# Merge gate products in three split passes, recurrent roots in pairs, and splits moved, in a two-layer diffusion step

## The reference, cut to what is computed

```
h = rmsnorm(x) * (1 + scale1) + shift1
q, k, v, xr, gr, ga, gb = split(h @ w_in)
att = attention(q, k, v)                  # 8 heads of 128; latent: band plus context keys; a sink
xc = conv4(xr)
for d in (forward, backward):
    r = sigmoid(block_diag(xc, wa) + ba);  i = sigmoid(block_diag(xc, wx) + bx)
    log_a = -8 * r * softplus(-lambda)
    u = sqrt(1 - exp(2 * log_a)) * (i * xc)
    y_d = scan(h = exp(log_a) * h + u)
merged = sigmoid(ga) * (att @ w_attn_proj) + sigmoid(gb) * ((gelu(gr) * (y_0 + y_1)) @ w_rnn_proj)
x = x + gate1 * (merged @ w_out)
x = x + gate2 * moe(rmsnorm(x) * (1 + scale2) + shift2)      # 16 experts, top 2 in one group
```

## Time and profile before

| | us |
|---|---|
| median of 3 runs | 1554.89 (1554.48 to 1556.72) |
| the profiled execution, its own time | 1553.74 |
| its span, first to last instruction | 1551.9 |
| mean granted clock of TensorE | 0.992 of full speed |

### The profile page before, as it was taken

The page is one execution under the profiler, slowest core; times in us unless marked ns, Lnnn a source line. Parts: engine busy times, 40 slices in busy tenths (PEclk is TensorE's granted clock), DMA queues, the critical chain, the costliest instruction groups (busy, mean ns, idle before and its releaser), DMA issues.

```text
span 1551.9 us, 19505 instructions
## 1 busy us (share of the span) xinstructions
PE 1493.8 (96%) x7383; PEld 1192.0 (77%) x7383; DVE 1116.6 (72%) x1717; ACT 921.5 (59%) x1176; POOL 161.2 (10%) x218
## 2 busy tenths in 40 slices
PE   6999999999998999999999999999999899999996
PEld 4699866669875788888769988666999478888885
DVE  4447656774646999999873665677564789999986
ACT  1323569982224887778752355999321578778774
POOL 0100012200011000000240000221000201000002
PEclk9999999999999999999999999999999999999999
DMA  9455433216547999999855644112340799999983
GB/s 350 172 193 198 154 112 105 75 57 217 217 167 277 361 402 408 408 408 406 318 193 173 214 165 164 63 64 89 134 141 32 301 354 407 413 411 410 407 348 123
DMA packets 132708, 373.01 MB, mean 240 GB/s; under 512 B 9216, under 2 KB 12672, under 8 KB 132608
## 3 DMA queue, kind: packets, MB, share of 16 engines
q1 hardware_dynamic: 113728, 326.57, 55.9%
q0 software_dynamic: 10432, 25.18, 4.6%
q10 hardware_dynamic: 8448, 19.94, 3.3%
HBM read 351.71 MB, written 19.94 MB: 239 GB/s over the span
## 4 chain that ended last, share of the span: by engine, by line
PE 81%; DVE 6%; ACT 5%; DMA 4%; issue 3%; POOL 1%; SPq 0%; POOLq 0%; ACTq 0%; DVEq 0%
PE bank L551 24%; PE bank L864 21%; PE bank L870 11%; PE bank L540 10%; PE bank L561 2%; DMA ring<-in_w_ada 2%; PE bank L836 2%; PE bank L749 2%; PE bank L722 1%; PE bank L577 1%; PE bank L659 1%; PE bank L654 1%; PE bank L570 1%; PE bank L908 1%; PE bank L973 1%
## 5 line engine op out<-in xcount | busy, mean ns | idle before, releaser
L1915 DVE TENSOR_TENSOR spot_low<-spot,piece_high 128x2048 fp32r<-128x2048 f32 x192 | 433.5, 2287 | 31.5 <-ACT piece_high L1279 30.1
L1279 ACT ACTIVATE piece_high<-spot 128x2048 fp32r<-128x2048 f32 x192 | 366.6, 1917 | 42.4 <-PE bank L870 40.2
L864 PE MATMUL bank<-piece_high,ga_r 128*128 128x512 f32 x768 | 308.7, 402 | 2.9 <-ACT ga_r L1296 1.4
L864 PE MATMUL bank<-spot_low,ga_r 128*128 128x512 f32 x768 | 301.7, 393 | 0.0
L870 PE MATMUL bank<-piece_high,ga_r 128*128 128x512 f32 x768 | 210.7, 396 | 0.0
L551 PE MATMUL bank<-parts_r,ga_r 128*128 128x384 f32 x768 | 202.6, 345 | 0.0
L540 PE MATMUL bank<-hT,ring 128*128 128x384 f32 x544 | 184.9, 494 | 4.3 <-ACT ga L1221 2.3
L864 PEld LDWEIGHTS bank<-piece_high,ga_r 128*128 128x128 f32 x768 | 144.3, 188 | 37.8 <-ACT ga_r L1284 2.2
L870 PEld LDWEIGHTS bank<-piece_high,ga_r 128*128 128x128 f32 x768 | 144.3, 188 | 34.6
L864 PEld LDWEIGHTS bank<-spot_low,ga_r 128*128 128x128 f32 x768 | 144.6, 188 | 30.7
L540 PEld LDWEIGHTS bank<-hT,ring 128*128 128x128 f32 x544 | 102.1, 193 | 71.0 <-issue 3.9
(11 more groups left out here) (317 smaller groups left out, 2337.4 us busy)
## 6 DMA issues: line engine op xcount, KB each, us to landing
spot<-in_w_gate_up SPq DMA_DIRECT2D x128, 1024.0 KB, 8.0
spot<-in_w_down SPq DMA_DIRECT2D x64, 1024.0 KB, 8.0
ring<-in_w_ada SPq DMA_DIRECT2D x24, 2048.0 KB, 8.6
ring<-in_w_in SPq DMA_DIRECT2D x22, 2048.0 KB, 8.2
expert_rows<-gb ACTq DMA_DIRECT2D x28, 512.0 KB, 6.9
ring<-in_w_attn_proj SPq DMA_DIRECT2D x4, 2048.0 KB, 7.9
ring<-in_w_rnn_proj SPq DMA_DIRECT2D x4, 2048.0 KB, 12.5
ring<-in_w_out SPq DMA_DIRECT2D x4, 2048.0 KB, 7.8
```

The lines of the kernel that those rows point to most:

```text
L864: pe.matmul(out[n], high[:, 2 * q + k, :], w[:, k, n * 512:(n + 1) * 512], start=(q == 0 and k == 0 and i == 0), stop=False)
L1279: ac.activation(highs[p % HIGHS], spots[u], ACT.Copy).then_inc(S("piece_high"), 1)
L1915: ve.tensor_tensor(spots_low[u], spots[u], highs[p % HIGHS].bitcast(F32), ALU.subtract)\
```

## The change

- ga and gb join `SPLIT` between gr and ap, so all 24 products of the loop are split products. high_part and low_part are now issued in every iteration of the loop, two products ahead, the first two of ap included.
- The high parts get new homes, listed one by one in `HIGH_HOMES`: three pieces of the tile gb (G0 to G2), spare, two pieces of the tile xc (X0, X1, free once 6 and 12 scans are done), and three pieces of `parts` (A0 to A2). A high part waits for the product that last used its home.
- The root goes by 1 - a*a = (1 + a)^2 * tanh(-log_a / 2), so sqrt = (1 + a) * sqrt(tanh(.)). The square on ACT and one_minus_square on DVE go; the factor (a + 1) is applied in scan, after the root.
- The roots are taken in pairs: `lru_root(i-10)` and `lru_root(i-9)` in even iterations only.
- The scan is moved from number i-9 to number i-10 in iteration i; the last two are made in the ap stage.
- Attention's output is split into `hT_r` and `qT_r` (its own place), as is the merged output. The recurrent output is no longer split in scan but by `rnn_split` in the ap stage, into `parts_r[:, 1]` and `gr_r`.

```diff
-SPLIT = [(kind, n) for kind in ("q", "xr", "gr", "ap", "rp", "wo") for n in range(KT)]
+SPLIT = [(kind, n) for kind in ("q", "xr", "gr", "ga", "gb", "ap", "rp", "wo") for n in range(KT)]
-LATE_HIGHS = 4
+LATE = 5 * KT
+HIGH_HOMES = (["G0", "G1", "G2"] * 2 + ["G0", "G1"]
+              + ["G2", "spare", "G2", "spare", "G2", "X0", "spare", "X0"]
+              + ["X1", "spare", "X0"] + (["A0", "A1", "A2", "spare"] * KT)[:3 * KT - 3])
+SCANS_OF_HOME = {"X0": 6, "X1": 12}
+def home_user_ahead(at):
+    same = [b for b in range(EARLY, at) if HIGH_HOMES[b - EARLY] == HIGH_HOMES[at - EARLY]]
+    return same[-1] if same else None
+RNN_SPLIT_AT = {2: (0,), 3: (1, 2), 4: (3,), 5: (4, 5), 6: (6,), 7: (7,)}
...
 PE, loop
-                    if kind == "gr":
-                        split_product(l, kind, i, parts_r[:, 0], parts_r[:, 1])
-                    else:
-                        product((l, kind, i % KT), s, i % 4, h_all)
+                    split_product(l, kind, i % KT, parts_r[:, 0], parts_r[:, 1])
...
-                for name, high, low in (("ap", parts_r[:, 0], parts_r[:, 1]), ("rp", qT_r, gr_r),
-                                        ("wo", parts_r[:, 0], parts_r[:, 1])):
+                for name, high, low in (("ap", hT_r, qT_r), ("rp", parts_r[:, 1], gr_r), ("wo", hT_r, qT_r)):
...
 ACT, high_part
-                    if at >= EARLY + LATE_HIGHS:
-                        ac.wait_ge(S("gemm_done"), G_AT[(l, *SPLIT[at - LATE_HIGHS])] + 1)
-                    elif at > EARLY:
+                    if at >= EARLY and home_user_ahead(at):
+                        ac.wait_ge(S("gemm_done"), G_AT[(l, *SPLIT[home_user_ahead(at)])] + 1)
+                    elif at >= EARLY and HIGH_HOMES[at - EARLY] in SCANS_OF_HOME:
+                        ac.wait_ge(S("lru_used"), l * 16 + SCANS_OF_HOME[HIGH_HOMES[at - EARLY]])
+                    elif at >= LATE:
                         ac.wait_ge(S("gemm_done"), G_AT[(l, "gb", KT - 1)] + 1)
...
 ACT, lru_tables and lru_root
-                    link(ac.activation(a, a, ACT.Exp, bias=c_log[0], scale=c_log[0]))
-                    if m:
-                        ac.wait_ge(S("lru_square"), m)
-                    ac.activation(a2, a, ACT.Square).then_inc(S("lru_act"), 1)
+                    ac.activation(a, a, ACT.Exp, bias=c_log[0], scale=c_log[0]).then_inc(S("lru_act"), 1)
-                    ac.wait_ge(S("lru_square"), l * 16 + n + 1)
+                    ac.wait_ge(S("lru_act"), l * 16 + n + 1)
...
 ACT, loop and after it
-                    if i == 3 * KT - 1:
-                        high_part(EARLY)
-                    if i > KT:
+                    if i > KT and i % 2 == 0:
+                        lru_root(i - KT - 2)
                         lru_root(i - KT - 1)
-                    if i + AHEAD < KT:
-                        high_part(2 * KT + i + AHEAD)
+                    high_part(2 * KT + i + AHEAD)
...
-                high_part(EARLY + 1)
                 lru_tables(15)
+                high_part(LATE + AHEAD)
+                lru_root(14)
                 lru_root(15)
...
 DVE, scan
-                    link(ve.scalar_tensor_tensor(ti, ti, 1.0, xc[:, j, :], ALU.add, ALU.mult))
+                    ve.wait_ge(S("lru_act"), m + 1)
+                    ve.scalar_tensor_tensor(ti, ti, 1.0, xc[:, j, :], ALU.add, ALU.mult)
                     ve.wait_ge(S("root_ready"), m + 1)
+                    link(ve.scalar_tensor_tensor(th, a, 1.0, th, ALU.add, ALU.mult))
                     link(ve.tensor_tensor(th, th, ti, ALU.mult))
...
-                        halves(qT_r[:, j, :], gr_r[:, j, :], gr[:, j, :]).then_inc(S("rnn_ready"), 1)
...
+                def rnn_split(j):
+                    if j == 0:
+                        ve.wait_ge(S("gemm_done"), G_AT[(l, "gb", KT - 1)] + 1)
+                    halves(parts_r[:, 1, j, :], gr_r[:, j, :], gr[:, j, :]).then_inc(S("rnn_ready"), 1)
...
 DVE, loop and ap stage
-                    if i + AHEAD < KT:
-                        low_part(2 * KT + i + AHEAD)
-                    if i > KT:
-                        one_minus_square(i - KT - 1)
-                        scan(i - KT - 1)
-                low_part(EARLY)
+                    low_part(2 * KT + i + AHEAD)
+                    if i > KT + 1:
+                        scan(i - KT - 2)
                 att_split(HEADS - 1)
-                low_part(EARLY + 1)
-                one_minus_square(15)
-                scan(15)
                 for n in range(KT):
-                    low_part(EARLY + n + AHEAD)
+                    low_part(LATE + n + AHEAD)
+                    if n < 2:
+                        scan(14 + n)
+                    for j in RNN_SPLIT_AT.get(n, ()):
+                        rnn_split(j)
```

More of the change, by code:

```diff
@@ L293, in build @@
         actT = gaf[:, 2048:2560].rearrange("p (k c) -> p k c", k=4)
-        parts_r, qT_r, gr_r = sb_r("parts"), sb_r("qT"), sb_r("gr")
+        parts_r, qT_r, gr_r, hT_r = sb_r("parts"), sb_r("qT"), sb_r("gr"), sb_r("hT")
         flat_r = lambda name: sb_r(name)[:, :, :].rearrange("p k t -> p (k t)")
-        hTf, xcf, gaf_r, gbf_r, spare_r = flat_r("hT"), flat_r("xc"), flat_r("ga"), flat_r("gb"), sb_r("spare")
+        xcf, gaf_r, gbf_r, spare_r = flat_r("xc"), flat_r("ga"), flat_r("gb"), sb_r("spare")
         flat_parts_r = parts_r[:, :, :, :].rearrange("p i k t -> p (i k t)")
@@ L301, in build @@
         w_parts = [(part(gaf_r, i), part(gbf_r, i)) for i in range(PAIRS_OF_PARTS)]
-        late_high = [part(spare_r, 0)] + [part(hTf, i) for i in range(LATE_HIGHS - 1)]
+        high_home = {"spare": part(spare_r, 0)}
+        for i in range(3):
+            high_home[f"G{i}"], high_home[f"A{i}"] = part(gbf_r, i), part(flat_parts_r, i)
+        for i in range(2):
+            high_home[f"X{i}"] = part(xcf, i)
         ring_r = sb_r("ring")
@@ L383, in w_high_part @@
             at = SPLIT_AT[kind, n]
-            return w_parts[at % PAIRS_OF_PARTS][0] if at < EARLY else late_high[at % LATE_HIGHS]
+            return w_parts[at % PAIRS_OF_PARTS][0] if at < EARLY else high_home[HIGH_HOMES[at - EARLY]]
         def w_low_part(l, kind, n):
@@ L729, in _ @@
                     kind = ("gr", "ga", "gb")[i // KT]
-                    if i % 4 == 0 and kind != "gr":
-                        s = weights(l, kind + str(i % KT // 4))
                     scores(i)
-                    if kind == "gr":
-                        split_product(l, kind, i, parts_r[:, 0], parts_r[:, 1])
-                    else:
-                        product((l, kind, i % KT), s, i % 4, h_all)
+                    split_product(l, kind, i % KT, parts_r[:, 0], parts_r[:, 1])
                     if i % 4 == 0 and i <= KT:
@@ L1071, in high_part @@
                     ac.wait_ge(S(f"w_loaded{s}"), 16 * (use + 1))
[L1072 to L1074 removed]
+                    if at >= EARLY and home_user_ahead(at):
[3 more added lines that the diff above has]
+                    elif at >= LATE:
                         ac.wait_ge(S("gemm_done"), G_AT[(l, "gb", KT - 1)] + 1)
[L1076 removed]
+                    elif at >= PAIRS_OF_PARTS:
                         ac.wait_ge(S("gemm_done"), G_AT[(l, *SPLIT[at - PAIRS_OF_PARTS])] + 1)
@@ L1229, in _ @@
                 att_copy(23)
-                high_part(EARLY + 1)
                 lru_tables(15)
+                high_part(LATE + AHEAD)
+                lru_root(14)
                 lru_root(15)
-                for at in range(EARLY, len(SPLIT)):
-                    if at + AHEAD < len(SPLIT):
+                for at in range(LATE, len(SPLIT)):
+                    if LATE < at < len(SPLIT) - AHEAD:
                         high_part(at + AHEAD)
-                    if at == EARLY:
+                    if at == LATE:
                         ada_copy(l, 10)
@@ L1485, in softplus @@
                 ve.tensor_scalar(sp_(6), sp_(2), -4.0, None, ALU.mult)
-                ve.tensor_scalar(sp_(7), sp_(2), 4.0, None, ALU.mult)
+                ve.tensor_scalar(sp_(7), sp_(2), 2.0, None, ALU.mult)
                 ve.tensor_scalar(hb[:, 0, :, :], vec[:, :, 1, 0:16], 0.5, None, ALU.mult)
@@ L1638, in softmax_norm @@
                         .then_inc(S("probs_ready"), 1)
[L1640 to L1644, removed]
                 def scan(n):
@@ L1698, in att_split @@
                     if h == 0:
-                        ve.wait_ge(S("gemm_done"), G_AT[(l, "gr", KT - 1)] + 1)
-                    halves(parts_r[:, 0, h, :], parts_r[:, 1, h, :], qT[:, h, :]).then_inc(S("att_split"), 1)
+                        ve.wait_ge(S("gemm_done"), G_AT[(l, "vl", 1)] + 1)
+                    halves(hT_r[:, h, :], qT_r[:, h, :], qT[:, h, :]).then_inc(S("att_split"), 1)
+                def rnn_split(j):
+                    if j == 0:
+                        ve.wait_ge(S("gemm_done"), G_AT[(l, "gb", KT - 1)] + 1)
+                    halves(parts_r[:, 1, j, :], gr_r[:, j, :], gr[:, j, :]).then_inc(S("rnn_ready"), 1)
```

(6 more changed lines are left out.)

## The result

The changed kernel takes 1600.95 us (median of 4 runs, 1599.95 to 1603.35), the kernel before on the same chip 1555.81 (4 runs, 1554.48 to 1558.61): ratio 1.0299, 95% interval 1.0280 to 1.0317. It is slower by 45 us; 1600 was predicted. The profiled run has a span of 1599.0 us against 1551.9.

A forecast was written before the change was run, and what follows sets the result against it. PE was taken to set the pace, ACT right behind. Per layer +27 - 1.8 + 0.5 - 2.0 - 0.5 = +23, two layers +46, on 1553.7 gives 1600 us; range 1578 to 1640.

The forecast's parts named there:

- Part 3: Loop from i = 10: gate functions wait for the later scan, so ACT and DVE take turns; loss 27 us per layer.
- and behind low_part: DVE's queue in the loop: the scan runs behind the weights' remainder as well as one iteration later; no separate size.
- The covers: PE's about 7.0 us per iteration fits into 10.2, busy about 70%; ap-stage scans and splits, 29 of 34 us, are hidden.
- The recurrent output's split: Moved to ap, hidden until its last split, behind rp 0's remainder; between 1 us gain and 2 loss, gain 0.5 taken.
- The gain in i = 8 and 9: Two loop iterations with no wait for a scan yet, where the cheaper product was to gain 1.8 us per layer.
- The splits in 6 and 7: Weights of ga 0 and 1 split ahead of a softmax_max on DVE: 1.1 us, of which 0.5 was charged.
- The tail behind exps(23): From the last exps to the first ap product: 10.25 us was to become about 8.2, a gain of 2.0.
- The signs: Profile after: gate functions idle 2 us or more, exps 10.6 and 9.5 to 10 apart, about 32 fewer table loads.
- (a): Rival, loop: engines overlap after all and PE sets the pace, 1520 us; needs a round below 8.1 us; chance 0.12.
- (b): Rival, even iterations: both table loads on the path, 1.3 us longer each, 18 us in all, 1618 us; chance 0.09.
- (c): Rival, loop: PE's pauses lower its clock and PE sets the pace; about 1640 us, up to 1699; chance 0.10.
- (d): Rival, loop: gain and loss cancel at a round trip of about 8.3 us, time within 0.2%; chance 0.03.

The follow-up runs named there:

- e1: The changed kernel with the scan ahead of the weights' remainder (low_part) on DVE: 1554.97 us, 0.9997 of the kernel before.
- e2: The changed kernel with single roots and the scan one iteration earlier, as before the change; split products stay: 1587.24 us, ratio to the kernel before 1.0202.
- e5: The changed kernel with the gate functions issued right behind the next exps instead of ahead of it: 1625.04 us, ratio to the kernel before 1.0450.
- e4: The changed kernel with unused matmuls filling PE's pauses ahead of the turned probabilities from i = 9 on: 1604.70 us, ratio to the kernel before 1.0314.
- e8: e1 with the rounded weight copy made by DVE instead of ACT in seven even iterations, 10 to 22: 1545.56 us, 0.9937 of the kernel before.
- e7: e1 with gate functions behind the next exps and the remainder one iteration later, between softmax_max and softmax_norm: 1564.88 us, 1.0067 of the kernel before.

## Why the prediction was right

**The time** is right, and by its own terms: the loop was to cost 27 us per layer and costs 26.6 and 27.0. Even iterations of 384 keys were walked at 10.6 us and take 10.54 and 10.55, or 10.33 with 128 keys (10.4 walked); odd ones without a split 9.30 and 9.51 (9.3 and 9.5), with a split 10.14 (10.1). What made this possible is that each link was taken start to start from a row of before, and that nothing on PE lay in it.

**The cause was named half right.** Part 3 put the decision on the scan's move to one iteration later, with the gate functions that wait for it. In e1 the scan is just as late and the kernel loses nothing; in e2 it isn't late and 32 of the 45 us are lost; in e5 the gate functions no longer wait and 24 us more are lost. What decides is the other half of my sentence, "and behind low_part": the remainder waits for a copy that ACT makes after exps, and whatever DVE has queued behind it, scan and next softmax_max, starts only then, while ACT needs one or the other to go on. The shift sets which of the two closes the ring, and makes it longer: 10.15 us per iteration in place of e2's 9.46. Part 3's numbers were those of the right ring; its heading was not.

**The covers** held. PE was on no link of the chain in the loop. It was busy 80% of it, not about 70%: 8.1 us per iteration where 7.0 was taken. That goes with the low clock, since e1, at 0.98 in the first layer's loop, has 7.2. The recurrent output's split did end behind the landing of the rp weights: in the chain of the kernel after, L1559 is the last split and L1567 the remainder of rp 0 ahead of it,

```profile
382.16 13.42 DMA ring<-in_w_rnn_proj
...
396.70 1.22 DVE ring_r L1567
...
400.69 0.57 DVE gr_r L1559
```

and yet first ap product to logits is 0.5 and 0.8 us shorter, where a gain of 0.5 was taken.

**Small terms.** The gain in i = 8 and 9 was 2.3 us rather than 1.8. The product is 0.94 us cheaper in each by the chain (4.22 for 5.16), which makes 1.9. Most of the other 0.4 comes at the end: before, the chain reached exps(10) through ACT's gate functions, 1.78 us behind the start of product 10; in the kernel after it goes through softmax_max, and it is 1.45. The splits in 6 and 7 cost 0.8 rather than 0.5. The tail behind exps(23) gained 1.85 in the second layer (2.0 foreseen) and 0.2 in the first, where the clock was low.

**The signs** that the prediction named were there: the first gate function waits for DVE 2.0 to 5.0 us, exps follow each other at 10.54 and 9.3 to 10.1 us in turn, and the loops have 30 table loads in place of 62.

**The rivals.** (a), overlap, needed a round of less than 8.1 us; it is 10.15 on average. (b), both table loads on the path: the timeline of ACT in the kernel after has the second load behind the copy, beside DVE's remainder,

```profile
264.65 1.28 ACT L1201 ACT_TABLE_LOAD   x1
265.95 0.94 ACT L1201 ACTIVATE tmp<-tmp 128x387 f32<-128x387 f32 x2
266.79 1.04 ACT L1094 ACTIVATE gb_r<-ring 128x1024 fp32r<-128x1024 f32 x1
267.85 1.28 ACT L1230 ACT_TABLE_LOAD   x1
```

and the root starts 1.30 us after its load does. The Trainium skill ("ScalarE: Activation LUTs", What ACT_TABLE_LOAD costs) puts a switch at 2.66 us; the trace doesn't agree, here as before. (c), the clock: it fell (0.91 and 0.95 in the two loops), and e4 shows that the loop doesn't feel it. (d), cancelling, is what e1 does.

**Where the expected gain went.** The split product is 0.91 us cheaper, 29 us for all. It is had only while PE sets the pace, in i = 8 and 9. From i = 10 on even the best order found (e8) gives 105.2 to 105.7 us, which is the kernel before's 104.9 to 105.3: ACT and DVE with their hand-overs set that pace, and what e8 gains lies outside this loop. Its profiled execution, the slowest of its six (the median is 9.5 us below before's), has a span 5.2 us below before's; its two layers are 4.1 and 3.4 us shorter from exps(6) to the logits, by i = 8 and 9 (2.3 each), the tail (1.8 each) and the stretch to the logits (0.7 and 0.9), less 0.8 each in i = 6 and 7 together and 0.8 in the second loop.

## What to carry to other kernels

Before adding an operation to an engine's queue, ask what it waits for and what is queued behind it: an operation that waits for the other engine's work of this iteration, put ahead of one that the other engine needs, turns two engines side by side into two that take turns, whatever their busy shares say. Put what the others wait for first and what waits for others last; here the swap of two calls was worth 45 us. And when a ring is opened, walk the next one through all engines, PE's banks too, before believing the gain; once PE is on the path, the low clock that comes with its pauses costs time too (e7).

## What the runs showed of the hardware

DVE rounds the same 128x1024 weights faster than ACT. The group of the rounded copies of DVE in e8, beside ACT's copies at 1053 ns in the earlier trace rows:

```profile
L1577 DVE CAST gb_r<-ring 128x1024 fp32r<-128x1024 f32 x10 | 6.9, 685 | 0.3 <-PE bank L569 0.3
```

A copy of 685 ns is little over half of the remainder's 1222 ns on the same engine.

The granted clock fell within the loop of the kernel after, where PE is busy 80% and pauses in every iteration. The four gate matmuls (L762) took 1.47 us in some iterations and 2.79 in others, near the ratio of the levels of 1.2 and 2.4 GHz. The pause right before doesn't decide which. Two iterations of the same kernel, with the turned probabilities (L727) behind the pause and the gates behind them:

```profile
235.01 0.52 PE L727 MATMUL bank<-con,pr 128*128 128x128 f32 x3 [1.94 <-DVE pr L1647]
235.37 1.47 PE L762 MATMUL bank<-xc,gatew 128*128 128x387 f32 x4
...
1011.77 0.73 PE L727 MATMUL bank<-con,pr 128*128 128x128 f32 x3 [1.94 <-DVE pr L1647]
1012.29 2.79 PE L762 MATMUL bank<-xc,gatew 128*128 128x387 f32 x4
```

Both follow a pause of 1.94 us. A pause of 3.22 us was followed by 2.79, one of 2.45 us once by 1.47 and once by 2.64. What else the clock depends on, these runs don't show.
